# Attention on one core: six chunks of transposes in one group, values behind the second scores, paired reciprocals, sinks written once

## What is computed

```python
s = jnp.einsum('bnqgrd,bnkgd->bngrqk', qb, kb).astype(jnp.float32)
s = jnp.where(valid, s + alibi, -jnp.inf)
p = jax.nn.softmax(jnp.concatenate([s, sink_logit], axis=-1), axis=-1)[..., :-1]
o = jnp.einsum('bngrqk,bnkgd->bnqgrd', p, vb)
```

## Time and profile before

| what | value |
|---|---|
| median of 3 runs | 731.63 us (731.01 to 731.79) |
| profiled execution, its own time | 729.93 us |
| span of its trace | 728.1 us |
| busy: PE, DVE, ACT, POOL | 703.9, 507.8, 389.6, 322.6 us |
| stretch of the attentions | about 162 to 283 us of the span |
| mean granted TensorE clock | 0.995 |

### The profile page before, as it was taken

How to read it: one execution, slowest core, us unless ns; L and a number is a source line. 1 busy time by engine, 2 the same in 40 slices (tenths; PEclk the granted TensorE clock), 3 DMA queues, 4 the chain that set the end, 5 groups by cost and what they waited for, 6 DMA issues and landing times.

```text
span 728.1 us, 10269 instructions
## 1 busy us (share of the span) xinstructions
PE 703.9 (97%) x3761; PEld 510.4 (70%) x3761; DVE 507.8 (70%) x813; ACT 389.6 (54%) x586; POOL 322.6 (44%) x243
## 2 busy tenths in 40 slices
PE   7999999999999999999999999999999999999973
PEld 7888888886775556888888766666666666666631
DVE  5646422215988887214387998888888888888977
ACT  6500000104888887001122688888888888888815
POOL 2433458953778771610001444444444444442213
PEclk9999999999999999999999999999999999999998
DMA  9422112100500003705666599999999999999978
GB/s 308 141 59 59 32 56 59 30 0 22 124 1 2 1 1 136 211 2 203 230 224 227 180 370 387 388 386 384 383 385 382 390 386 383 383 386 380 392 267 345
DMA packets 62515, 158.06 MB, mean 217 GB/s; under 512 B 10184, under 2 KB 25008, under 8 KB 62464
## 3 DMA queue, kind: packets, MB, share of 16 engines
q1 hardware_dynamic: 55728, 139.58, 52.9%
q0 software_dynamic: 6432, 17.21, 7.0%
q10 hardware_dynamic: 304, 0.59, 0.2%
HBM read 142.69 MB, written 18.87 MB: 222 GB/s over the span
## 4 chain that ended last, share of the span: by engine, by line
PE 86%; DMA 5%; DVE 4%; SPq 1%; issue 1%; ACT 1%; POOL 0%; DVEq 0%; POOLq 0%
PE ps L1021 7%; PE ps L1028 7%; PE ps L1031 7%; PE ps L731 6%; PE ps L730 6%; PE ps L729 6%; PE ps L833 4%; PE ps L895 4%; PE ps L897 4%; PE ps L896 4%; PE ps L1054 4%; PE ps L1050 4%; PE ps L1058 4%; PE ps L818 3%; PE ps L857 3%; DMA wd<-in_expert_w_down 3%
## 5 line engine op out<-in xcount | busy, mean ns | idle before, releaser
L1833 DVE TENSOR_TENSOR wgulo<-wgu,unit 128x2048 fp32r<-128x2048 f32 x64 | 146.3, 2287 | 26.6 <-ACT unit L1291 26.6
L1291 ACT CAST unit<-wgu 128x2048 fp32r<-128x2048 f32 x64 | 122.2, 1909 | 1.8 <-DVE eid L1794 0.9
L2126 POOL DMA_INDIRECT expert_rows<-ysb,idx x32 | 71.5, 2236 | 106.7 <-ACT ysb L1344 97.3
L2119 POOL DMA_INDIRECT xg<-h_rows,idx x32 | 58.6, 1833 | 68.1 <-PE ps L990 58.6
L729 PE MATMUL ps<-hThi,whi 128*128 128x512 f32 x200 | 78.4, 392 | 0.0
L731 PE MATMUL ps<-hThi,wlo 128*128 128x512 f32 x200 | 78.0, 390 | 0.0
L730 PE MATMUL ps<-hTlo,whi 128*128 128x512 f32 x200 | 77.9, 390 | 0.0
L1839 DVE TENSOR_TENSOR wdlo<-wd,unit 128x2048 fp32r<-128x2048 f32 x32 | 73.1, 2285 | 2.3 <-ACT unit L1300 2.2
L1021 PE MATMUL ps<-unit,xThi 128*80 128x512 f32 x256 | 70.9, 398 | 0.2 <-ACT xThi L1312 0.2
L1028 PE MATMUL ps<-unit,xTlo 128*80 128x512 f32 x256 | 69.2, 392 | 0.0
L1031 PE MATMUL ps<-wgulo,xThi 128*80 128x512 f32 x256 | 69.2, 391 | 0.0
(11 more groups left out here) (231 smaller groups left out, 1448.9 us busy)
## 6 DMA issues: line engine op xcount, KB each, us to landing
wgu<-in_expert_w_gate SPq DMA_DIRECT2D x64, 512.0 KB, 11.8
wgu<-in_expert_w_up SPq DMA_DIRECT2D x64, 512.0 KB, 14.8
wd<-in_expert_w_down SPq DMA_DIRECT2D x32, 1024.0 KB, 17.0
y<-expert_rows SPq DMA_DIRECT2D x16, 512.0 KB, 10.6
wraw<-in_w_in SPq DMA_DIRECT2D x14, 512.0 KB, 3.8
xin<-in_x SPq DMA_DIRECT2D x8, 512.0 KB, 6.7
x<-in_x SPq DMA_DIRECT2D x8, 512.0 KB, 7.1
out<-fo SPq DMA_DIRECT2D x8, 512.0 KB, 3.9
```

The costliest lines, as they stand in the source:

```text
L1291: nc.scalar.copy(weight_unit(e, a)[:], raw_half(wgu, e, a)).then_inc(ahi_done, 1)
L1833: nc.vector.tensor_tensor(raw_half(wgulo, e, a), raw_half(wgu, e, a), weight_unit(e, a)[:].bitcast(F32), ALU.subtract).then_inc(alo_done, 1)
```

## The change

- `attention_plan`: `lag` is 12 without an offset. In na the chunks of step `s` stand at ticks `4*s + 13`, `14`, `15` and its values at `4*s + 19`. In swa the three chunks of a step with `g` 1 stand at `4*s + 13`, `13`, `14`, and those of the next block's step with `g` 0 at the same stretch's second to third tick, so that six chunks stand behind one group of scores. The block's values stand at the tick of the following group of scores.
- `by_vector`: in swa DVE copies every second chunk, where it was every third.
- Reciprocals are taken for two units in one instruction, at odd ticks, for the units `u - 3` and `u - 2`; the multiplications on DVE follow there.
- The buffers of swa have 386 columns per head and the sinks stand in the last, which the exponential reads and does not write: bias goes to one column above where the probabilities go. The sinks are written for the first four swa steps alone.

```diff
-    lag = 8
+    lag = 12
...
-        for c0 in range(0, nc_, GROUP):
-            group = range(c0, min(c0 + GROUP, nc_))
-            items += [("T", s, c) for c in group]
-            items += late
-            late = [("V", s, c) for c in group] if kind == "na" or g == 1 else []
...
-            ticks[4 * s + 3 + lag + (4 * j) // len(items)].append(it)
+        if kind == "na":
+            places = [4 * s + lag + j for j in (1, 2, 3)]
+        elif g == 1:
+            places = [4 * s + lag + j for j in (1, 1, 2)]
+        else:
+            places = [4 * (s - 1) + lag + j for j in (2, 3, 3)]
+        for c in range(nc_):
+            ticks[places[c]].append(("T", s, c))
+        for c in range(nc_ if kind == "na" or g == 1 else 0):
+            ticks[4 * s + lag + (7 if kind == "na" else 4)].append(("V", s, c))
...
-            return n % 2 == 0 if n < na_chunks else n % 3 == 0
+            return n % 2 == 0
...
-                buf = pbuf(u)
+                probs, logits_ = pbuf(u), biased(u)
                 if s >= NA_STEPS:
-                    buf = pswa[s % 4][:, u % 4, 0:1 + steps[s][4]]
-                nc.scalar.activation(buf, buf, ACT.Exp, bias=mneg[:, u:u + 1], scale=-1.0,
+                    first = 3 * P - steps[s][4]
+                    probs, logits_ = pswa[s % 4][:, u % 4, first:3 * P + 1], pswa[s % 4][:, u % 4, first + 1:3 * P + 2]
+                nc.scalar.activation(probs, logits_, ACT.Exp, bias=mneg[:, u:u + 1], scale=-1.0,
...
                         if s >= NA_STEPS + 4:
                             dve.wait_ge(tr_done, chunk_no[(s - 4, last_chunk[s - 4])] + 1)
-                        nc.vector.tensor_copy(pswa[s % 4][:, :, 0], nsink[:, 4 * g:4 * g + 4]).then_inc(sink_set, 1)
-                        dve.wait_ge(sink_set, 2 + s - NA_STEPS)
+                        else:
+                            nc.vector.tensor_copy(pswa[s % 4][:, :, 3 * P + 1], nsink[:, 4 * g:4 * g + 4]).then_inc(sink_set, 1)
+                            dve.wait_ge(sink_set, 2 + s - NA_STEPS)
...
-            def reciprocal(u):
-                dve.wait_ge(exp_done, u + 1)
-                nc.vector.reciprocal(esum[:, u:u + 1], esum[:, u:u + 1]).then_inc(recip_done, 1)
+            def reciprocals(u):
+                dve.wait_ge(exp_done, u + 2)
+                nc.vector.reciprocal(esum[:, u:u + 2], esum[:, u:u + 2]).then_inc(recip_done, 2)
+
+            def normalised(u):
+                dve.wait_ge(recip_done, u + 1)
+                nc.vector.tensor_scalar(pbuf(u), pbuf(u), esum[:, u:u + 1], None, ALU.mult).then_inc(norm_v, 1)
...
-                if 0 <= u - 2 < NU:
-                    reciprocal(u - 2)
-                    if norm_by_vector(u - 2):
-                        dve.wait_ge(recip_done, u - 1)
-                        nc.vector.tensor_scalar(pbuf(u - 2), pbuf(u - 2), esum[:, u - 2:u - 1], None, ALU.mult).then_inc(norm_v, 1)
+                if 0 <= u - 3 < NU and u % 2 == 1:
+                    reciprocals(u - 3)
+                for x in (u - 3, u - 2) if u % 2 == 1 else ():
+                    if 0 <= x < NU and norm_by_vector(x):
+                        normalised(x)
```

More of the change, by code:

```diff
@@ L64 @@
 MIX_FROM = 8
-GROUP = 3
 LAST_QUERIES = (4, 8)
@@ L99, in attention_plan @@
             steps.append(("swa", b, g, lo * P, (hi - lo) * P))
-    lag = 8
+    lag = 12
     ticks = [[] for _ in range(4 * len(steps) + lag + 4)]
-    late = []
     for s, (kind, i, g, k0, nk) in enumerate(steps):
         nc_ = -(-nk // P)
-        items = []
-        for c0 in range(0, nc_, GROUP):
-            group = range(c0, min(c0 + GROUP, nc_))
-            items += [("T", s, c) for c in group]
-            items += late
-            late = [("V", s, c) for c in group] if kind == "na" or g == 1 else []
-        if s == len(steps) - 1:
-            items += late
-        for j, it in enumerate(items):
-            ticks[4 * s + 3 + lag + (4 * j) // len(items)].append(it)
+        if kind == "na":
[8 more added lines that the diff above has]
+            ticks[4 * s + lag + (7 if kind == "na" else 4)].append(("V", s, c))
     return steps, ticks
@@ L198, in encoder @@
         pna = [at(f"pna{i}", [P, 4, 3 * P], F32, H + 32 * KB + i * 6 * KB) for i in range(4)]
-        pswa = [at(f"pswa{i}", [P, 4, 3 * P + 1], F32, off) for i, off in enumerate((H + 56 * KB, TD + 8 * KB, TMP, Q + 8 * KB))]
+        pswa = [at(f"pswa{i}", [P, 4, 3 * P + 2], F32, off) for i, off in enumerate((H + 56 * KB, TD + 8 * KB, TMP, Q + 8 * KB))]
         ptna = [at(f"ptna{i}", [P, 5, 512], F32, W + 4 * KB + i * 10 * KB) for i in range(2)]
@@ L437, in pbuf, with biased @@
                 return pna[s % 4][:, u % 4, 0:steps[s][4]]
-            return pswa[s % 4][:, u % 4, 1:1 + steps[s][4]]
+            return pswa[s % 4][:, u % 4, 3 * P - steps[s][4]:3 * P]
+        def biased(u):
+            s = u // 4
+            if s < NA_STEPS:
+                return pbuf(u)
+            return pswa[s % 4][:, u % 4, 3 * P + 1 - steps[s][4]:3 * P + 1]
         def sbank(u):
@@ L1535, in bias_and_max @@
                     nc.vector.tensor_tensor_reduce(
-                        out=pbuf(u), in0=ps[:, sbank(u), 0:nk], in1=tab, scale=-(HD ** -0.5), scalar=BIG, op0=ALU.add, op1=ALU.min,
+                        out=biased(u), in0=ps[:, sbank(u), 0:nk], in1=tab, scale=-(HD ** -0.5), scalar=BIG, op0=ALU.add, op1=ALU.min,
                         accum_out=mneg[:, u:u + 1]).then_inc(bias_done, 1)
@@ L1543, in bias_and_max @@
                             dve.wait_ge(tr_done, chunk_no[(s - 4, last_chunk[s - 4])] + 1)
-                        nc.vector.tensor_copy(pswa[s % 4][:, :, 0], nsink[:, 4 * g:4 * g + 4]).then_inc(sink_set, 1)
-                        dve.wait_ge(sink_set, 2 + s - NA_STEPS)
+                        else:
+                            nc.vector.tensor_copy(pswa[s % 4][:, :, 3 * P + 1], nsink[:, 4 * g:4 * g + 4]).then_inc(sink_set, 1)
+                            dve.wait_ge(sink_set, 2 + s - NA_STEPS)
                     first = (k0 // P) - (i - 1)
                     nc.vector.tensor_tensor_reduce(
-                        out=pbuf(u), in0=ps[:, sbank(u), 0:nk], in1=dist[:, first * P:first * P + nk],
+                        out=biased(u), in0=ps[:, sbank(u), 0:nk], in1=dist[:, first * P:first * P + nk],
                         scale=SLOPES[hh], scalar=nsink[:, hh:hh + 1], op0=ALU.add, op1=ALU.min,
                         accum_out=mneg[:, u:u + 1]).then_inc(bias_done, 1)
-            def reciprocal(u):
-                dve.wait_ge(exp_done, u + 1)
-                nc.vector.reciprocal(esum[:, u:u + 1], esum[:, u:u + 1]).then_inc(recip_done, 1)
+            def reciprocals(u):
[4 more added lines that the diff above has]
+                nc.vector.tensor_scalar(pbuf(u), pbuf(u), esum[:, u:u + 1], None, ALU.mult).then_inc(norm_v, 1)
             def wo_split(k):
```

## The result

The changed kernel takes **736.15 us** (median of 4, 735.86 to 736.87) where the one before takes 731.32: ratio 1.0076, 95% interval 1.0064 to 1.0088. It is slower by 4.8 us; forecast were 736.0 us and +4.4.

What follows compares the result with a forecast made beforehand. It took PE to bound the kernel, so any attention delay delays the end. Terms +0.4, +2.4 and +1.6 sum to +4.4 us: 734.3 for the profiled execution, median 736.0 as that execution lies 1.7 below; range 732.8 to 739.2.

Steps and rivals of the forecast that it cites:

- The full block: Sliding window, one block from scores to scores: 10.12 us instead of 9.43, because chunks 4 to 6 wait for copies.
- the multiplication beside POOL: DVE's multiplication in a full block: 0.62 us beside a busy POOL; with 0.34 as low end the block takes 9.84.
- that case: Rival, chance 0.10: DVE's multiplication waits out POOL's 1.24 us, third bias 0.6 us later in every block, +3 us, 739.
- The late exponentials: ACT, full block: a step's last two exponentials wait behind the result's copy, starting 0.57 and 1.18 us after the first scores.
- ACT's gap of 1.42 us: Sign in the profile after: ACT idle before the result's copy until PE ends the wait, some 1.4 us in a block.
- the rival of PE's pace: Rival, chance 0.10: copies keep up, a full block takes 8.50 us, total 727.8; chunk 1's copy must start by about 2.2.
- The sum: Whole kernel: +4.4 us, 734.3 for the profiled execution's 729.93, hence a forecast median of 736.0; chance 0.70.
- (a): Fill and hand-over between the mixers, step 5's to step 14's scores: 37.2 us against 36.80, +0.4; nothing to +1.4 possible.
- (b): Four sliding-window blocks, step 14 to step 22: 40.5 us against 38.12, +2.4; +1.2 with the short multiplication, +3.6 with unseen waits.
- (c): Last half block, step 22's scores to the projection: +1.6 us, bounds +0.7 and +2.2.
- Work taken away: DVE: twelve sink copies (0.20 us each) and half of 96 reciprocals (0.08 each) removed; gain covered or small.
- The pairs' price of nothing in a full block: DVE's paired reciprocal just does not wait for the late exponential (1.94 against 1.99); pairs cost 0.4 us in the last block.

Runs made afterwards that it cites:

- run 10: The kernel before with the pairs of reciprocals alone: 732.13 us, ratio 1.0020 to the kernel before, full block 9.81 us.
- run 1: The changed kernel with the sliding window's result copy on ACT behind the fourth exponential again: 736.64 us, full block 9.92 us.
- run 3: The changed kernel with the sliding window's chunk copies on ACT ahead of the exponential and its result copy behind the fourth exponential: 731.49 us, full block 8.73 us.
- run 5: The changed kernel with chunk copies ahead of exponentials, sliding-window result copy behind the fourth, neighbourhood result copy ahead of the next: 728.43 us, ratio 0.9966 to the kernel before.
- run 4: The changed kernel with the neighbourhood attention's result copy on ACT ahead of the next exponential: 734.12 us, ratio 1.0040 to the kernel before.
- run 8: The kernel of run 5 with the sliding window's chunk copies ahead of the exponential from its first step, not only from step 12: 728.34 us.
- run 9: The kernel before with the sinks' part of the change alone: 729.95 us, ratio 0.9992, full block 9.40 us.
- mended order: The changed kernel's order with ACT's three places put right, as in run 5, also called the mended kernel: 728.43 us, full block 8.73 us.
- run 7: The kernel of run 5 with the sinks written for every step again: 730.51 us, ratio 0.9995 to the kernel before, full block 8.93 us.
- run 12: The changed kernel with single reciprocals again: 736.91 us, ratio 1.0085 to the kernel before, full block 9.92 us.
- run 6: The kernel of run 5 with single reciprocals again: 729.94 us, ratio 0.9992 to the kernel before, full block 8.73 us.

## Why the prediction was right, and where it was not

**The full block** was walked through the lists and came out nearly place by place. Offsets from the first scores (248.32 in the rows above):

| | forecast | measured |
|---|---|---|
| first, second bias | 0.95, 1.47 | 0.95, 1.49 |
| multiplication | 2.21 | 2.22 |
| copy of chunk 2 on DVE | 2.83 | 2.63 |
| third bias | 3.43 | 3.24 |
| copy of chunk 1 on ACT | 3.01 | 3.01 |
| copy of chunk 3 on ACT | 4.68 | 4.50 |
| chunk 6, second scores | 5.31, 5.90 | 5.12, 5.71 |
| next block | 10.12 | 9.92 |

The one term that was off is the multiplication beside POOL: 0.34 instead of 0.62, taken from the one row that was 0.70 long. With 0.34 the walk gives its low end, 9.84. The other 0.08 to the measured 9.92 is a hand-over that the walk left out: the copy of chunk 2 needs the chunk, and PE has it ready 2.63 us behind the scores, 0.07 later than DVE gets there. So the measured path comes from PE's first two chunks, and the biases and the multiplication, with which the forecast path began, just miss being on it.

POOL was at work in both places, so POOL being at work is not the condition. It depends on where in one of POOL's multiplications DVE's begins. The row of 0.70 in the kernel before began 0.76 us behind the start of this one of POOL's, which ends at 242.14:

```profile
240.90 1.24 POOL L2073 TENSOR_SCALAR pswa<-pswa,esum 128x384 f32<-128x384 f32 x1
```

and ended 0.21 behind its end, at 242.36; the four others of 0.70 in that kernel, and seven of 0.77 in run 10, lie likewise, 0.69 to 0.76 us behind a start and 0.21 over the end. Those that begin 0.39 to 0.54 behind the start of one of POOL's of the same size keep their 0.42. In the changed kernel's full block DVE's begins 0.06 ahead of POOL's; then it keeps its 0.42 and POOL's takes 1.47. The rule of the Trainium skill that such a pair shares its port exclusively (SBUF, Who interferes with whom) would have had the multiplication wait for the whole of one of POOL's; that case had 0.10 and didn't come, and the longest in any trace here is 0.77. The traces agree with that rule in part: a multiplication that begins late in one of POOL's waits out the rest of it, one that begins 0.39 to 0.54 us into it doesn't. POOL's own six took 7.88 us instead of 7.44: four take 1.24 and two 1.47, and these two are the ones that begin while a multiplication on DVE is under way.

**The late exponentials** were forecast where they are and ACT's gap of 1.42 us too. That they hold only chunk 4, and not the block, was in the walk and is what run 1 shows; run 3 adds that they cost 0.18 us once the copies are moved. The sign given for the rival of PE's pace, chunk 1 copied by about 2.2, was not tried by itself: in runs 3 and 5 that copy starts at 2.2 and a block takes 8.73, but there chunk 3's copy is moved too.

**The sum** was right in size by errors that cancel. The terms, from the scores' starts in the two traces:

| | forecast | measured |
|---|---|---|
| (a) step 5 to step 14 | +0.4 | 40.03 - 36.80 = +3.2 |
| (b) step 14 to step 22 | +2.4 | 39.67 - 38.12 = +1.6 |
| (c) step 22 to the projection | +1.6 | 20.97 - 19.65 = +1.3 |

(a) is the step that failed, outside its bound of +1.4. It had 0.3 us for waits of chunks and of products "that wait for the result's copy behind an exponential". In the changed kernel's trace these products wait four times, 0.39, 0.51, 0.32 and 1.26 us, 2.5 in all; run 4 takes three of the waits away, halves the last, and gets 2.35 us back. So the mechanism was named and mis-sized. Behind the scores of step 8 the first bias starts 1.13 us after them (203.57; the sinks' copy ahead of it is 0.36 long), its exponential 0.53 later, the result's copy 0.51 behind that and the product another 0.49 later, at 2.66, where PE was ready at 2.15. It isn't so in every step: the values of steps 2, 3 and 6 follow with 0.14 us of a gap or less. What run 4 leaves, +0.9 against the kernel before, lies between steps 10 and 14 (16.15 us against 15.28), where the two mixers meet; 0.67 of it is the last of the four waits, and run 8 shows that shortening it only moves it.

That 736.0 was met to 0.2 us is luck. The sum was made for the profiled execution and gave it +4.4; it measured +6.9, of which the three terms are 6.1. The median moved by 4.8 only, because the two profiled executions lay on different sides of their medians.

**Work taken away** "is covered or small": for the sinks this holds for a full block in the order before (run 9) and not in the mended order (run 7), where a block gets 0.20 longer with them. The pairs' price of nothing in a full block holds (run 12). The Trainium skill's advice for smaller instructions where an engine makes others wait (Perfetto Trace Analysis, Optimizing Scalar/DVE Operations) is borne out in one order and not in the other: with single reciprocals the kernel before is 1.5 us faster than with pairs (run 10), the mended kernel 1.5 us slower (run 6), and the changed kernel the same (run 12). In run 10 the rows put it down to where the multiplication lands; in run 6 the cause is open.

What stays open: why single executions of one kernel differ by up to 3 us (728.6 to 732.0 for the kernel before beside run 6), the part of run 6 that the trace doesn't show, and how far DVE's own list, with the third bias behind a copy, could be mended in the changed kernel.

## What to carry to other kernels

When work is regrouped on the bounding engine, walk every list that frees its buffers, with start-to-start times from the rows, up to the last copy that the group needs: here the group saved 0.3 us of a block and put two exponentials ahead of the copies that it needed. In an in-order list an operation whose input is ready belongs ahead of one whose input is only just being made: chunk copies stood behind exponentials whose scores were new, and two old exponentials behind a result's copy whose values weren't done. Putting the three places right turned 0.8% slower into 0.3% faster, with the pairs and the sinks' part in it. A saving on a helper engine is worth little while a wait behind it stays, and a removed or moved instruction may have been filling that wait.

## What the runs showed that I had not expected

- Pairing reciprocals made the kernel before slower by 0.2% (1.0020, 1.0007 to 1.0033), with fewer instructions; its rows show a gap of 0.41 us on DVE that the multiplication had filled before. That the gap is the cause is read from the rows, not isolated by a run.
- The multiplication on DVE beside a busy POOL took 0.34 us of DVE in the changed kernel's block and 0.62 in one place of the kernel before, while POOL's six took 7.88 and 7.44 us. Which of the two gives way, and by how much, goes by where in the other's instruction it begins.
- Sinks written once gained 0.03 us of a full block in the kernel before and 0.20 in the mended order.
- Two repairs that were worth 0 and 1.01 us a block alone were worth 1.19 together.
